# Differential heads gathered with the queries on the partitions, normed there and then transposed

## The chip, the core and the metric

The kernel runs on one core of a Trainium2 chip. The metric is the device time of one execution in microseconds (us), the median of several runs. All arithmetic is float32, with TensorE products made from pairs of rounded float32 parts.

## The reference

Three model blocks run on one sequence of 512 tokens with a width of 1024. The change lies in the second block, which has two layers; each layer is a feed-forward part, a mixer with attention, and another feed-forward part. The mixer has eight plain heads ("fox", eight of width 64, worked in four pairs) and four differential heads of width 128. What matters is this:

```python
p_d = jax.nn.softmax(s_d, axis=-1)
a_d = p_d[:, :, 0] - lam * p_d[:, :, 1]
o_d = jnp.einsum('bhqk,bhkd->bhqd', a_d, v_d)
...
o_d = _rmsnorm(o_d, subln) * (1.0 - lambda_init)
# y = x * rsqrt(mean(x * x, axis=-1) + 1e-5) * gain: the mean is over the 128 values of one head and one query
return jnp.concatenate([o_f, o_d], axis=-1) @ w_out
```

## The kernel before

The activations are held transposed: features on the 128 partitions, the 512 tokens along the free dimension. Each weight is loaded by DMA, rounded by ScalarE (L1579), and its remainder made by GpSimd (L2662); each product is then three matmuls (L1183 to L1185, `products`). The work is one order written out by hand: `program` calls the same sequence of steps on each engine, and each engine's class emits its own instructions of a step, with semaphore waits between the engines. So every engine has one queue in a fixed order, and a waiting instruction holds all that stands behind it on its engine.

PSUM is eight banks, and a step takes the bank that was taken or let go the longest time ago among those not held. `take` on an engine waits for the event `free` of the bank's former user. A bank that a head's output is gathered in (`('o', layer, 'd', i)`) is held from its first gather to its fourth and then let go, so that it goes to the end of the turn.

`attend` runs 32 jobs in each layer, a head and one of its four blocks of 128 queries: first the four differential heads, then the four pairs of fox heads. One pass of its loop emits, in this order, the scores of one job (L1484, L1487; two banks taken ahead of both), one gather, DVE's weighing of an earlier job, one turn (the transposes at L1497 and ScalarE's copy, L1879), and one step of `both()` (two for a pair). A step of `both()` is a step of `projections()` and then a step of `norms()`. A step of `projections()` is half a projection (`T_part`); behind the second half DVE evicts the projection with `fox_in` (L2502, L2503) or `diff_in`.

`norms()` norms the differential heads. Call the pass in which the fourth gather of head i is emitted **pass A**, and those behind it **B** and **C**. Before the change, a head goes so:

- Pass A: the gather (L1511) gives values on the partitions and queries along the bank. ScalarE copies the bank to `OD` (L1887) and frees it; then `diff_norm` j = 0, ScalarE's square of `OD` (L1901).
- Pass B: j = 1 (`roots`). TensorE sums the squares over the partitions with four matmuls of two columns (L1239), ScalarE takes the root (L1619), DVE the reciprocal (L2113). DVE's part stands behind `fox_in`.
- Pass C: j = 2 (`row`). TensorE spreads the result over all partitions with four matmuls of 128 columns (L1269), and ScalarE copies them out (L1634).
- The pass behind C: j = 3. DVE multiplies `OD` by the row and the gain (L2563) and by a constant (L2565).

Later ScalarE and DVE split `OD` into its rounded part and remainder (`diff_parts`), and the output projection reads them.

Of the kernel before, what the change touches and what calls it, by code (L numbers as in the profile page):

```python
# [7 lines left out]
ALU = mybir.AluOpType  # L8
# [733 lines left out]
def second(on, k, layer, before):  # L742
    L, A = (str(layer), before.A)
    scale = before.sum if layer else before.twin
    prior = ('added', 'f2_0', 7) if layer else ('final', 'fin1', 7)
    res = Residual('f1_' + L, lambda j: 0.5, banked(Sum('m' + L, k.R[1 - layer], S, prior, (), 2, [('lo', ('mid', 'f1_' + L), FF - 1)])), scale=scale, A=k.XA('m' + L), g=lambda j: param(k, 'mix_' + L, j))
    ffn(on, k, Ffn('f1_' + L, 'f1i' + L, 'f1o' + L, A, scale, res, [('filled', ('d', 'f2_0', 7))] if layer else [('filled', ('d', 'ff1', 7))], None if layer else before, iter(()) if layer else before.side))
    last = ('filled', ('d', 'f1_' + L, 7))
    A, R = (res.A, res.sum)
    on.mix_loads(L, last)  # L750
    on.T2((('ff', L), 'ff' + L, 0), (('dqk', L, 0), 'dqk' + L, 0), A)
    on.roots(R, 2)
    on.T(('dqk', L, 4), 'dqk' + L, 4, A)
    on.row(R, hold=True)
    on.diff_in(L, 0, R, last)
    on.diff_in(L, 4, R, last)
    on.forget(L, R, last)
    for kp in range(4):
        on.K(('dv', L), 'dv' + L, 0, A, kp, 4)
        if kp in (1, 2):  # L760
            on.rope(L, 4 * kp - 4)
    for tt in range(4):
        on.mix_value(L, 'dv', k.DV, tt, R, last)
    for n in (1, 5):
        on.T(('dqk', L, n), 'dqk' + L, n, A)
        on.diff_in(L, n, R, last)
    on.mix_lambda(L, layer)
    for kp in range(4):
        on.K(('fv', L), 'fv' + L, 0, A, kp, 4)
        if kp < 2:  # L770
            on.rope(L, 4 * kp + 1)
    for tt in range(4):
        on.mix_value(L, 'fv', k.FV, tt, R, last)
    at = Heads(k, L, [('d', i) for i in range(4)] + [('f', i) for i in range(4)], k.P2, [last, ('lambda', L), ('forgot', L)])
    at.OA, at.lam, at.scale = (Pair('oa' + L, k.OAH, k.OAL), k.sm[:, 68:69], 1.0 - (0.8 - 0.6 * math.exp(-0.3 * layer)))
    at.old = [('filled', ('s', L, ('d', 3), 3, 1)), ('filled', ('o', L, 'd', 3))]
    at.cleared = ('lo', 'oa' + L, 7)
    res = Residual('out2_' + L, lambda j: 1.0, banked(Sum('f2_' + L, k.R[layer], S, ('added', 'f1_' + L, 7), (1, 3, 5, 7), 0, [('filled', ('out2_' + L, 0))])), A=k.XA('f2_' + L), g=lambda j: param(k, 'ffn2_' + L, j))

    def projections():  # L780

        turn = None
        for n in (2, 6, 3, 7):
            on.T_part(('dqk', L, n), 'dqk' + L, n, A, 0, 2)
            if turn is not None:
                on.rope(L, turn)
            yield
            on.T_part(('dqk', L, n), 'dqk' + L, n, A, 1, 2)
            on.diff_in(L, n, R, last)
            turn = n  # L790
            yield
        for n in (0, 4, 1, 5, 2, 6, 3, 7):
            on.T_part(('fqk', L, n), 'fqk' + L, n, A, 0, 2)
            if n == 0:
                on.rope(L, turn)
            yield
            on.T_part(('fqk', L, n), 'fqk' + L, n, A, 1, 2)
            on.fox_in(L, n, R, last)
            yield
        yield  # L800
        for i in range(4):
            on.diff_parts(at, i)
            if i % 2:
                yield
        for n in range(KT):
            on.T(('outd_' + L, n), 'out' + L, n, at.OA, kt=4, first=4)
            on.part(res, n, ('outd_' + L, n))
            yield
            yield

    def norms():

        for i in range(4):
            while at.out <= i:
                yield
            for j in range(4):
                on.diff_norm(at, j, i)
                yield

    def both():  # L820
        one, two = (projections(), norms())
        while next(one, 'end') != 'end':
            next(two, None)
            yield
    attend(on, at, both())
    for n in range(KT):
        on.T(('out2_' + L, n), 'out' + L, n, at.OA, kt=4)
        on.residual(res, n, ('out2_' + L, n), ('filled', ('fqk', L, 7)))
    A = res.A
    scale = res.sum  # L830
    nxt = banked(Sum('fin2' if layer else 'f1_1', k.R[1 - layer], S, ('fox', L, 7), range(8) if layer else (), 2, [('lo', ('mid', 'f2_' + L), FF - 1)]))
    if layer:
        twin = banked(Sum('n3', k.R[2], S, None, range(8)))
        twin.slots = nxt.slots
        res = Residual('f2_1', lambda j: 0.5, nxt, scale=scale, twin=twin, by='final2')
    else:
        res = Residual('f2_0', lambda j: 0.5, nxt, scale=scale, A=k.XA('f1_1'), g=lambda j: param(k, 'ffn1_1', j))
    ffn(on, k, Ffn('f2_' + L, 'f2i' + L, 'f2o' + L, A, scale, res, [('filled', ('out2_' + L, 7))]))
    return res
# [291 lines left out]
class Tensor(Engine):  # L1131
# [368 lines left out]
    def gather(self, at, h, qt):  # L1500

        k, e = (self.k, self.e)
        key, outs = (at.bank(h), at.outs(h, qt))
        bo = self.take(k.banks, *key, hold=True) if qt == 0 else self.bank(*key)
        for name, weights, place in outs:
            self.wait_ge('turned', name)
        for event in at.ready(h):
            self.wait_ge(*event)
        for kt in range(qt + 1):
            for c, (name, weights, (a, z)) in enumerate(outs):  # L1510
                m = e.matmul(bo[a:z, qt * 128:qt * 128 + 128], at.value(h, kt, c), at.T.of(name)[:, kt * 128:kt * 128 + 128], start=kt == 0, stop=kt == qt)  # L1511
        m.then_inc(*k.filled.inc(*[('free', name) for name, weights, place in outs], *([('filled', key)] if qt == 3 else [])))
        if qt == 3:
            k.banks.let(key)

    def diff_norm(self, at, j, i):
        sq = diff_sum(at, i)
        if j == 1:
            self.roots(sq, 2, 8.0)
        if j == 2:  # L1520
            self.row(sq)

    def lru(self, s, n, w=0):
        k, e = (self.k, self.e)
# [26 lines left out]
def conv_sum(k):  # L1551
    return Sum('cn', k.R[1], S, ('oscaled', 3), range(8))


def diff_sum(at, i):
    sq = Sum(('hn', at.tag, i), at.N.of(('hn', at.tag, i)))
    sq.last = 0
    return sq


class Scalar(Engine):
# [319 lines left out]
    def head_out(self, at, h):  # L1881
        k, e, key = (self.k, self.e, at.bank(h))
        kind, i = h
        if kind == 'd':
            self.wait_ge('filled', key)
            self.wait_ge('load', 'cum', at.tag)
            e.copy(k.OD[:, i, :], self.bank(*key)).then_inc(*k.act.inc(('od', at.tag, i), ('free', key)))  # L1887
        if kind == 'f':
            self.high(at.OA, i, self.bank(*key), ('filled', key), *at.old, *([at.cleared] if i > 1 else []))
        if kind == 'm':  # L1890
            pass
# [3 lines left out]

    def diff_norm(self, at, j, i):
        k, e = (self.k, self.e)
        if j == 0:
            m = self.take(at.N, 'hn', at.tag, i)
            self.wait_ge('od', at.tag, i)  # L1900
            e.activation(m, k.OD[:, i, :], ACT.Square).then_inc(*k.act.inc(('ssq', ('hn', at.tag, i), 0)))  # L1901
        if j == 1:
            self.roots(diff_sum(at, i), 2, 8.0)
        if j == 2:
            self.row(diff_sum(at, i))

    def diff_parts(self, at, i):
        self.high(at.OA, 4 + i, self.k.OD[:, i, :], ('diff normed', at.tag, i), *at.old)
# [124 lines left out]
class Vector(Engine):  # L2033
# [424 lines left out]
    def mix_lambda(self, L, layer):  # L2458
        k, e, o = (self.k, self.e, COL['lam_' + L][0])
        for j in range(2):  # L2460
            e.tensor_tensor(k.sm[:, 64 + j:65 + j], k.col[:, o + 2 * j:o + 2 * j + 1], k.col[:, o + 2 * j + 1:o + 2 * j + 2], ALU.mult).then_inc(*k.dve.inc(*([('lam products', L)] if j else [])))
        lam = k.sm[:, 68:69]
        self.wait_ge('lam exp', L)
        e.tensor_tensor(lam, k.sm[:, 67:68], k.sm[:, 66:67], ALU.subtract).then_inc(*k.dve.inc())
        self.settle()
# [89 lines left out]

    def diff_norm(self, at, j, i):
        k, e = (self.k, self.e)
        x, tag = (k.OD[:, i, :], ('hn', at.tag, i))
        if j == 1:
            self.roots(diff_sum(at, i), 2, 8.0)  # L2560
        if j == 3:
            self.wait_ge('row', tag)
            e.scalar_tensor_tensor(x, x, param(k, 'subln_' + at.tag), diff_sum(at, i).acc, ALU.mult, ALU.mult).then_inc(*k.dve.inc(('free', tag)))  # L2563
            self.settle()
            e.tensor_scalar(x, x, at.scale, None, ALU.mult).then_inc(*k.dve.inc(('diff normed', at.tag, i)))  # L2565

    def diff_parts(self, at, i):
        self.low(at.OA, 4 + i, self.k.OD[:, i, :])
# [266 lines left out]
```

## Time and profile before

| | |
|---|---|
| Runs | 3512.21, 3517.94, 3516.43 us; median 3516.43 us |
| Profiled execution | 3512.08 us, with a span of 3510.4 us from first to last instruction |
| Busy, share of the span | TensorE 98%, TensorE weight load 79%, DVE 35%, ScalarE 36%, GpSimd 42% |
| Chain that ended last | TensorE 93%, DVE 2%, ScalarE 2%, DMA 1%, issue 1%, GpSimd 1% |
| Heads of the first layer | head 0 copied out at 1719.8 us, head 3 at 1787.4 us |
| Heads of the second layer | head 0 copied out at 2725.1 us, head 3 at 2792.7 us |

A row of the timeline gives the start in us, the duration in us, the engine, the line, the operation, the output and input, and how many instructions were merged. In brackets stands how long the engine sat idle before it, and what released it. PE is TensorE's matmul part, PEld its weight load, ACT is ScalarE, POOL is GpSimd, `ps` is a PSUM bank and `t` a tile in SBUF. A float32 matmul at L1239, L1269 and L1511 leaves two records each, a transpose at L1497 one. The end of a TensorE record is modelled and overlaps the next one; from start to start is the true pace.

### The profile page before, as it was taken

The page shows a single profiled execution, that of the slowest core. Times are in us where ns is not written, and L with a number is a line of the kernel's source. Part 1 is how long each engine was busy: PE and PEld are TensorE (multiplying, and loading weights), DVE is VectorE, ACT ScalarE, POOL GpSimd, SP SyncE. Part 2 cuts the span into 40 slices and gives each one's busy share as a digit, 9 for nine tenths or more (in the row PEclk, how much of TensorE's full clock was granted, in tenths as well). Part 3 has the DMA queues.
Part 4 walks back from the last instruction along what each step waited for, and adds up shares of the span by engine and source line. Part 5 has one row for each costly group of instructions (what it writes and reads, how often), then busy time and mean ns, then how long its engine had stood idle before and what let it go on. Part 6 is the DMA issues. An engine that isn't in the chain of part 4 may idle for free.

```text
span 3510.4 us, 39172 instructions
## 1 busy us (share of the span) xinstructions
PE 3442.5 (98%) x16124; PEld 2774.4 (79%) x16124; DVE 1236.9 (35%) x2137; ACT 1255.6 (36%) x1924; POOL 1471.6 (42%) x672
## 2 busy tenths in 40 slices
PE   8999999999999999999999999999999999999998
PEld 5777887887888887887777888888887778888776
DVE  3265784533111144212553111111113652111544
ACT  4524323433322332223454222322223553222544
POOL 4222444554544444445423444444445224444332
PEclk9999999999999999999999999999999999999999
DMA  7211223442333323333112223233332122223211
GB/s 269 70 51 55 90 97 111 153 150 73 126 132 120 102 96 132 135 94 108 55 34 96 99 95 95 88 105 98 94 96 88 33 76 95 97 90 102 72 60 55
DMA packets 99294, 341.19 MB, mean 97 GB/s; under 512 B 11371, under 2 KB 11755, under 8 KB 98956
## 3 DMA queue, kind: packets, MB, share of 16 engines
q1 hardware_dynamic: 98352, 336.97, 28.9%
q8 instruction: 128, 2.10, 0.3%
q10 hardware_dynamic: 764, 1.72, 0.1%
q14 instruction: 50, 0.41, 0.0%
HBM read 336.02 MB, written 2.10 MB: 96 GB/s over the span
## 4 chain that ended last, share of the span: by engine, by line
PE 93%; DVE 2%; ACT 2%; DMA 1%; issue 1%; POOL 1%; SPq 0%; DVEq 0%; ACTq 0%
PE ps L1183 26%; PE ps L1185 25%; PE ps L1184 25%; PE ps L1202 2%; PE ps L1204 2%; PE ps L1203 2%; PE ps L1484 2%; PE ps L1511 1%; PE ps L1497 1%; PE ps L1399 1%; PE ps L1269 1%; POOL t L2662 1%; PE ps L1413 0%; PE ps L1239 0%; DMA t<-in_w_ada 0%
## 5 line engine op out<-in xcount | busy, mean ns | idle before, releaser
L2662 POOL TENSOR_TENSOR t<-t,t 128x1024 fp32r<-128x1024 f32 (+2 forms) x588 | 1361.2, 2317 | 1925.3 <-ACT t L1579 1924.3
L1183 PE MATMUL ps<-t,t 128*128 128x512 f32 (+1 forms) x4048 | 1607.7, 397 | 17.4 <-POOL t L2662 8.6
L1185 PE MATMUL ps<-t,t 128*128 128x512 f32 (+1 forms) x4048 | 1583.9, 391 | 0.0
L1184 PE MATMUL ps<-t,t 128*128 128x512 f32 (+1 forms) x4048 | 1579.7, 390 | 0.0
L1183 PEld LDWEIGHTS ps<-t,t 128*128 128x128 f32 x4048 | 764.0, 189 | 184.8 <-issue 17.5
L1185 PEld LDWEIGHTS ps<-t,t 128*128 128x128 f32 x4048 | 763.2, 189 | 167.5
L1184 PEld LDWEIGHTS ps<-t,t 128*128 128x128 f32 x4048 | 764.1, 189 | 157.9 <-issue 1.4
L1579 ACT CAST t<-t 128x1024 fp32r<-128x1024 f32 (+2 forms) x588 | 584.3, 995 | 571.6 <-PE ps L1185 416.3
L2455 DVE TENSOR_TENSOR t<-t,ps 128x512 f32<-128x512 f32 x110 | 75.7, 688 | 531.7 <-PE ps L1185 516.9
L1648 ACT CAST t<-t 128x512 fp32r<-128x512 f32 x158 | 97.0, 621 | 401.4 <-DVE t L2455 361.5
L1835 ACT ACTIVATE t<-t 128x512 f32<-128x512 f32 x88 | 55.6, 632 | 315.1 <-DVE t L2448 315.0
L2047 DVE TENSOR_TENSOR t<-t,t 128x512 fp32r<-128x512 f32 x138 | 120.1, 875 | 119.7 <-ACT t L1648 119.7
L2290 DVE SCALAR_TENSOR_TENSOR ps<-t,t,ps 128x392 f32<-128x392 f32 (+14 forms) x232 | 159.0, 685 | 6.2
L2416 DVE TENSOR_TENSOR t<-ps,t 128x512 f32<-128x512 f32 x32 | 22.1, 692 | 381.5 <-PE ps L1185 381.5
L2448 DVE TENSOR_TENSOR t<-ps,t 128x512 f32<-128x512 f32 x88 | 60.7, 690 | 251.4 <-PE ps L1185 225.5
L1202 PE MATMUL ps<-t,t 128*128 128x512 f32 x336 | 137.3, 409 | 6.6 <-DVE t L2151 3.9
L1872 ACT ACTIVATE t<-ps,t 128x128 f32<-128x128 f32 (+3 forms) x160 | 86.5, 545 | 151.7 <-PE ps L1497 66.2
L1204 PE MATMUL ps<-t,t 128*128 128x512 f32 x336 | 132.9, 396 | 0.0
L1203 PE MATMUL ps<-t,t 128*128 128x512 f32 x336 | 132.7, 395 | 0.0
L2511 DVE TENSOR_REDUCE t<-ps 128x1 f32<-128x128 f32 (+3 forms) x160 | 77.6, 485 | 72.9 <-PE ps L1487 71.8
L1817 ACT ACTIVATE t<-t,t 128x512 fp32r<-128x512 f32 x48 | 34.7, 723 | 157.2 <-DVE t L2418 107.5
L2099 DVE SCALAR_TENSOR_TENSOR t<-t,t,t 128x1024 f32<-128x1024 f32 x49 | 77.2, 1575 | 31.5 <-DMA t<-in_w_ada 31.4
(285 smaller groups left out, 2283.2 us busy)
## 6 DMA issues: line engine op xcount, KB each, us to landing
t<-in_w_f1i SPq DMA_DIRECT2D x88, 512.0 KB, 3.3
t<-in_w_f2i SPq DMA_DIRECT2D x88, 512.0 KB, 3.3
t<-in_w_ada SPq DMA_DIRECT2D x72, 512.0 KB, 4.4
t<-in_w_ffi SPq DMA_DIRECT2D x44, 512.0 KB, 3.7
t<-in_w_f1o SPq DMA_DIRECT2D x32, 512.0 KB, 3.6
t<-in_w_f2o SPq DMA_DIRECT2D x32, 512.0 KB, 3.5
t<-in_w_gate SPq DMA_DIRECT2D x24, 512.0 KB, 4.0
t<-in_w_out SPq DMA_DIRECT2D x48, 256.0 KB, 2.6
```

Of the source, the lines that this page charges most:

```text
L1183: e.matmul(out, wh[:, at], X.hi[c][:, 0:N], start=c == first, stop=False)
L1184: e.matmul(out, wh[:, at], X.lo[c][:, 0:N], start=False, stop=False)
L1185: m = e.matmul(out, wl[:, at], X.hi[c][:, 0:N], start=False, stop=c == final)
L1202: e.matmul(out, X.hi[c][:, at], wh[:, w], start=c == 0, stop=False)
L1203: e.matmul(out, X.hi[c][:, at], wl[:, w], start=False, stop=False)
L1204: m = e.matmul(out, X.lo[c][:, at], wh[:, w], start=False, stop=c == 7)
L1579: e.copy(k.WH[:, n % NHL, 0:w], k.raw[:, j % NRAW, 0:w]).then_inc(*k.rounded.inc(('rounded', j)))
L1648: e.copy(A.hi[t], src).then_inc(*k.act.inc(('hi', A.tag, t)))
L1872: e.activation(p[:, 0:n], self.bank('s', *key)[:, 0:n], ACT.Exp, scale=at.root(h, qt, c) if h[0] == 'm' else 0.125, bias=st[:, 1:2], accum ...
L2047: e.tensor_tensor(A.lo[t], src, f(A.hi[t]), ALU.subtract).then_inc(*k.dve.inc(('lo', A.tag, t), *events))
L2290: e.scalar_tensor_tensor((c3 if j == 30 else a3)[:, :, lo:hi], h3[:, :, lo + w - 15:hi + w - 15], param(k, 'conv_w', w * 8 + i), a3[:, :, ...
L2662: e.tensor_tensor(k.WL[:, n % NHL, 0:w], k.raw[:, j % NRAW, 0:w], f(k.WH[:, n % NHL, 0:w]), ALU.subtract).then_inc(*k.rest.inc(('rest', j) ...
```

## The change

The gather of a differential head swaps its two operands, so that the queries are on the partitions and the 128 values of the head along the bank. The sum of squares of one query then runs along the free dimension: in pass A, instead of the copy, ScalarE makes four squares, one for each block of 128 queries, with an accumulated output, and takes the root at j = 0. In pass B (j = 1), where TensorE has no work any more, DVE takes the reciprocal and multiplies the PSUM bank by it into the scratch tile; this instruction frees the bank. In pass C (j = 2) TensorE transposes the scratch tile with four transposes, and ScalarE copies the result to `OD`, with the gain times the constant as its scale, once the load `cum` is done. The step j = 3 is gone. The product of gain and constant is one more small DVE instruction in each layer.

```diff
@@ second: norms()
-            for j in range(4):
+            for j in range(3):
@@ Tensor.gather
-                m = e.matmul(bo[a:z, qt * 128:qt * 128 + 128], at.value(h, kt, c), at.T.of(name)[:, kt * 128:kt * 128 + 128], start=kt == 0, stop=kt == qt)
+                turned, values = (at.T.of(name)[:, kt * 128:kt * 128 + 128], at.value(h, kt, c))
+                held, moved = (turned, values) if h[0] == 'd' else (values, turned)
+                m = e.matmul(bo[a:z, qt * 128:qt * 128 + 128], held, moved, start=kt == 0, stop=kt == qt)
@@ Tensor.diff_norm
-        sq = diff_sum(at, i)
-        if j == 1:
-            self.roots(sq, 2, 8.0)
+        k, e, tag = (self.k, self.e, ('hn', at.tag, i))
         if j == 2:
-            self.row(sq)
+            b, m = (self.take(k.banks, 'turned out', at.tag, i), at.N.of(tag))
+            self.wait_ge('od scaled', at.tag, i)
+            for t in range(4):
+                x = e.transpose(b[:, t * 128:t * 128 + 128], m[:, t * 128:t * 128 + 128], const(k, 'ident'))
+            x.then_inc(*k.filled.inc(('filled', ('turned out', at.tag, i)), ('free', tag)))
@@ Scalar.head_out
         if kind == 'd':
+            m, c = (self.take(at.N, 'hn', at.tag, i), self.take(k.cols, 'cols', ('hn', at.tag, i)))
             self.wait_ge('filled', key)
-            self.wait_ge('load', 'cum', at.tag)
-            e.copy(k.OD[:, i, :], self.bank(*key)).then_inc(*k.act.inc(('od', at.tag, i), ('free', key)))
+            for t in range(4):
+                w = slice(t * 128, t * 128 + 128)
+                e.activation(m[:, w], self.bank(*key)[:, w], ACT.Square, accum_out=c[:, t:t + 1]).then_inc(*k.act.inc())
@@ Scalar.diff_norm
+        tag = ('hn', at.tag, i)
         if j == 0:
-            m = self.take(at.N, 'hn', at.tag, i)
-            self.wait_ge('od', at.tag, i)
-            e.activation(m, k.OD[:, i, :], ACT.Square).then_inc(*k.act.inc(('ssq', ('hn', at.tag, i), 0)))
-        if j == 1:
-            self.roots(diff_sum(at, i), 2, 8.0)
+            c = k.cols.of(('cols', tag))[:, 0:4]
+            self.settle()
+            e.activation(c, c, ACT.Sqrt, scale=1.0 / 128, bias=unit(k, 2)).then_inc(*k.act.inc(('root', tag)))
         if j == 2:
-            self.row(diff_sum(at, i))
+            self.wait_ge('filled', ('turned out', at.tag, i))
+            self.wait_ge('load', 'cum', at.tag)
+            e.activation(k.OD[:, i, :], self.bank('turned out', at.tag, i), ACT.Copy, scale=k.sm[:, 69:70]).then_inc(*k.act.inc(('diff normed', at.tag, i), ('free', ('turned out', at.tag, i))))
@@ Vector.mix_lambda
+        e.tensor_scalar(k.sm[:, 69:70], param(k, 'subln_' + L), 1.0 - (0.8 - 0.6 * math.exp(-0.3 * layer)), None, ALU.mult).then_inc(*k.dve.inc())
@@ Vector.diff_norm
-        x, tag = (k.OD[:, i, :], ('hn', at.tag, i))
+        tag, key = (('hn', at.tag, i), at.bank(('d', i)))
         if j == 1:
-            self.roots(diff_sum(at, i), 2, 8.0)
-        if j == 3:
-            self.wait_ge('row', tag)
-            e.scalar_tensor_tensor(x, x, param(k, 'subln_' + at.tag), diff_sum(at, i).acc, ALU.mult, ALU.mult).then_inc(*k.dve.inc(('free', tag)))
+            c = k.cols.of(('cols', tag))[:, 0:4]
+            self.wait_ge('root', tag)
+            e.reciprocal(c, c).then_inc(*k.dve.inc())
             self.settle()
-            e.tensor_scalar(x, x, at.scale, None, ALU.mult).then_inc(*k.dve.inc(('diff normed', at.tag, i)))
+            e.tensor_tensor(halves(at.N.of(tag)), halves(self.bank(*key)), c.rearrange('p (a n) -> p a n', n=1).broadcast_to([128, 4, 128]), ALU.mult).then_inc(*k.dve.inc(('od scaled', at.tag, i), ('free', key), ('free', ('cols', tag))))
```

`settle` makes an engine wait for its own last instruction.

## Rows read from the trace of the kernel before

**Rows 1.** The page: busy time, share of the span and instructions of each engine.

```profile
PE 3442.5 (98%) x16124; PEld 2774.4 (79%) x16124; DVE 1236.9 (35%) x2137; ACT 1255.6 (36%) x1924; POOL 1471.6 (42%) x672
```

**Rows 2.** Windows: stretch, length, busy PE, PEld, DVE, ACT, POOL, TensorE clock, DMA.

```profile
1720.00:1735.00 15.00, 15.00 (x86) 11.16 (x86) 8.60 (x24) 9.50 (x19) 6.37 (x4) 1.00 0.12 36
```

**Rows 3.** Timeline: head 0 of layer 0, pass B, TensorE and DVE.

```profile
1726.48 0.39 PE L1185 MATMUL ps<-t,t 128*128 128x512 f32 x1
1726.71 0.95 PE L1239 MATMUL ps<-t,t 128*128 128x2 f32 x8
1726.91 0.68 DVE L2502 TENSOR_TENSOR t<-ps,t 64x512 f32<-64x512 f32 x1
1727.58 0.92 PE L1484 MATMUL ps<-t 64*128 64x384 f32 x4
1727.62 0.69 DVE L2503 TENSOR_TENSOR t<-ps,t 64x512 f32<-64x512 f32 x1
...
1728.34 0.20 DVE L2113 RECIPROCAL t<-t 128x8 f32<-128x8 f32 x1
```

**Rows 4.** Timeline: the row of head 0, then a turn of eight transposes.

```profile
1732.23 1.05 PE L1269 MATMUL ps<-t,t 128*128 128x128 f32 x8
...
1733.21 1.13 PE L1484 MATMUL ps<-t 64*128 64x512 f32 x4
...
1823.04 1.04 PE L1497 MATMUL ps<-t,t 128*128 128x128 f32 x8
...
1823.91 1.88 PE L1484 MATMUL ps<-t,t 80*128 80x512 f32 x4
```

**Rows 5.** Lines by form, 1700 to 1760 us: count, busy us, mean ns, idle before.

```profile
L2495 DVE TENSOR_TENSOR t<-ps,t 128x512 f32<-128x512 f32 x3 | 2.1, 692 | 5.2 <-PE ps L1474 5.2
```

**Rows 6.** Timeline: a release of TensorE by DVE in the third block.

```profile
3471.73 0.35 DVE L2533 TENSOR_SCALAR t<-t,t 128x256 f32<-128x256 f32 x1
...
3472.13 0.55 PE L1497 MATMUL ps<-t,t 128*128 128x128 f32 x3 [1.01 <-DVE t L2533]
```

**Rows 7.** Timeline: head 0 of layer 0, pass A, ScalarE.

```profile
1719.45 0.36 ACT L1872 ACTIVATE t<-ps,t 128x128 f32<-128x128 f32 x1
...
1719.79 0.59 ACT L1887 COPY t<-ps 128x512 f32<-128x512 f32 x1
...
1720.26 0.39 ACT L1879 COPY t<-ps 128x256 f32<-128x256 f32 x1
```

**Rows 8.** Timeline: head 3 of layer 0, passes B and C.

```profile
1794.66 0.20 DVE L2113 RECIPROCAL t<-t 128x8 f32<-128x8 f32 x1 [6.80 <-ACT t L1619]
...
1795.01 1.13 PE L1269 MATMUL ps<-t,t 128*128 128x128 f32 x8 [0.22 <-DVE t L2527]
...
1796.13 1.28 ACT L1872 ACT_TABLE_LOAD   x1 [1.50 <-DVE t L2517]
...
1798.14 1.53 PE L1484 MATMUL ps<-t,t 80*128 80x384 f32 x4 [1.34 <-ACT t L1872]
```

**Rows 9.** Timeline: TensorE's first matmuls behind waits elsewhere in the kernel.

```profile
1330.10 0.77 PE L1183 MATMUL ps<-t,t 128*128 128x512 f32 x1 [2.96 <-POOL t L2662]
...
1882.42 0.77 PE L1183 MATMUL ps<-t,t 128*128 128x512 f32 x1 [1.75 <-POOL t L2662]
...
1885.95 0.40 PE L1185 MATMUL ps<-t,t 128*128 128x512 f32 x1
...
2887.76 0.50 PE L1183 MATMUL ps<-t,t 128*128 128x512 f32 x1 [1.74 <-POOL t L2662]
...
3275.80 0.50 PE L1183 MATMUL ps<-t,t 128*128 128x512 f32 x1 [2.12 <-POOL t L2662]
...
3478.43 0.88 PE L1511 MATMUL ps<-t,t 128*64 128x128 f32 x12 [2.09 <-ACT t L1879]
```

**Rows 10.** Windows of TensorE alone: stretch, length, busy, clock, DMA share, GB/s.

```profile
1884.00:1886.00 2.00, 2.00 (x7) 0.53 0.53 207
...
3480.00:3482.00 2.00, 1.23 (x10) 0.50 0.02 4
```

More of the change, by code:

```diff
@@ L774, in second @@
     at = Heads(k, L, [('d', i) for i in range(4)] + [('f', i) for i in range(4)], k.P2, [last, ('lambda', L), ('forgot', L)])
-    at.OA, at.lam, at.scale = (Pair('oa' + L, k.OAH, k.OAL), k.sm[:, 68:69], 1.0 - (0.8 - 0.6 * math.exp(-0.3 * layer)))
+    at.OA, at.lam = (Pair('oa' + L, k.OAH, k.OAL), k.sm[:, 68:69])
     at.old = [('filled', ('s', L, ('d', 3), 3, 1)), ('filled', ('o', L, 'd', 3))]
@@ L1552, in conv_sum @@
     return Sum('cn', k.R[1], S, ('oscaled', 3), range(8))
[L1555 to L1558, printed above, removed]
 class Scalar(Engine):
```

## The prediction

> **What bounds the kernel now.** I read the page's busy times first. TensorE is busy for 98% of the span [rows 1], so the kernel is as long as TensorE's queue: an instruction taken off it is a gain of its pace, a wait put into it is a loss, and work on the other engines costs only where TensorE waits for it. Then I read the stretch of the differential heads by windows: TensorE 15.00 of 15.00 us busy at full clock, DVE 8.60, ScalarE 9.50 [rows 2]. The cover is complete there, so the norm costs today just what TensorE itself spends on it. Third came the timeline of one head, for the places in each queue. The eight heads (two layers of four) repeat one pattern; rows 3, 4 and 7 show head 0 of layer 0, and head 3 of a layer differs, as told below.
>
> **TensorE's own work.** Pass B loses the four two-column matmuls: from 1726.71 to the next scores at 1727.58, 0.87 us [rows 3]. In pass C the row takes 1733.21 - 1732.23 = 0.98 us, and eight transposes take 1823.91 - 1823.04 = 0.87, so four take 0.43 [rows 4]: -0.55. The gather has as many matmuls of 128x128 by 128 columns with its operands swapped: 0. If nothing waited, the change would give 8 x (0.87 + 0.55) = 11.4 us.
>
> Of the transposes a rule speaks against this. The Trainium skill (TensorE: Matmul & The Clock Gate, Part 4: PE-mode transpose) gives about 275 ns for one in a kernel; taken as a pace, four would cost 1.10 us by an estimate from that page and the new pass C would be no shorter than the old. The rows have eight in 0.87 us, because records overlap, so the sum keeps 0.43.
>
> **The bank's release.** Here is the new wait. Before, ScalarE's copy freed the output bank in pass A. Now DVE's product in pass B frees it. I followed the turn of the eight banks through the passes by the rule of the kernel: one of the eight is held by a projection and, from pass B on, one by the next head's output; between the fourth gather and the scores of pass C a head's passes take six or seven (a turn, a projection and for head 0 a rotation in A, two scores, the output and a turn in B), and in the old order the two-column matmuls took one more, for head 0 the freed bank itself. That taker is gone, so for heads 0, 1 and 2 the next taker of the output bank is one of the two score banks of pass C, and TensorE takes both ahead of its first scores matmul. Those scores are the very next thing in TensorE's queue behind the projection's last matmul, while DVE must first evict that projection (two `fox_in` instructions), then take the reciprocal, settle and multiply. All other engines' work stays behind TensorE's wait, and TensorE has nothing to run meanwhile.
>
> The wait, from head 0 [rows 3]: the projection's last matmul starts at 1726.48; TensorE reaches the scores at about 1726.71. DVE starts `fox_in` at 1726.91 and the reciprocal at 1728.34, ready at 1728.54. The product reads 512 columns from PSUM: nearest is DVE's product from PSUM of the same shape, 0.69 us [rows 5]. With 0.04 for settling it ends at 1729.27. DVE releases TensorE in 3472.13 - (3471.73 + 0.35) = 0.05 [rows 6]. So the scores start at 1729.33, against 1727.58 today: **+1.75 us** for each of these heads, with the 0.87 already counted in it. TensorE stands idle from 1726.48 + 0.39 to 1729.33, some 2.5 us. Below, the product can't be under the 0.35 of DVE's short product at L2533 [rows 6]: +1.4; above, nothing shown is over 0.2 more: +1.95.
>
> Six such heads: 6 x 1.75 = +10.5. Pass C of all eight: 8 x -0.55 = -4.4.
>
> **Head 3.** Its bank is next taken by its own transposes, which wait for the same product anyway: no new wait. It loses the 0.87. And today DVE stands 6.80 us at its reciprocal, since ScalarE's root comes late behind the turn copies; through that, the next `Exp` with its table load of 1.28 comes late and TensorE waits 1.34 at the scores, and 0.22 before the row [rows 8]. With the root moved to pass A, right behind the squares, DVE isn't held: both waits go. Two heads: 2 x -(0.87 + 1.34 + 0.22) = -4.9. If what is late next (the turn copies, which wait for the gather) keeps 1.34, it is only -2.2.
>
> **ScalarE.** The copy takes 1720.26 - 1719.79 = 0.47 of its queue; four squares from PSUM with an accumulator are nearest to the `Exp` of 128 columns, 1719.79 - 1719.45 = 0.34 apart [rows 7]: 1.36, so +0.9. Bounds are 0.34 each or, not overlapped, 0.36 plus an accumulator read of some 0.2: up to 2.2. The weight rounding and the turn copies behind it come 0.9 us later. The copy is first wanted by a gather two passes on, and the rounding by a projection two weights on, each several us away: 0, and 1 us a head if that cover fails. The root's table load moves with the root from B to A and the reload for `Exp` from C to B, both beside TensorE; the count stays. From 1719.79 the squares, a turn copy and a rounding (together under 3 us) and the load and root (1.28 and some 0.3) make the root ready by about 1724.5, and DVE comes to it at 1728.34: 0. The scaled copy in pass C replaces the row's copy: 0. `cum` is loaded long before: 0.
>
> **DVE and the rest.** The two products of j = 3, about 1.2 us a head, go from DVE, which is not the bound: 0. The extra scalar product in `mix_lambda` is 0. No DMA is added or moved, on SP's or any other queue, and GpSimd's queue keeps its instructions.
>
> Sum so far: 10.5 - 4.4 - 4.9 = **+1.2 us**.
>
> **The clock.** A TensorE that stands idle comes back at half clock in some places. Behind 1.75 us it ran from 1882.42 to 1885.95 for eight matmuls that at full pace (0.23 apart, [rows 3]) take 1.84: 1.7 us lost [rows 9], and the granted clock is 0.53 there, the 1.2 GHz level [rows 10]. So it was behind 2.09 (clock 0.50, [rows 9, 10]) and 2.96. Behind 1.74 and 2.12 it kept 2.4 GHz: first matmul 0.50 long instead of 0.77 [rows 9]. The idle time here is 2.5, between these; three of the five fell, and both that kept it were shorter. I take four of six: 4 x 1.7 = +6.8. Bounds are none (0) and six (+10.2).
>
> **Sum.** 1.2 + 6.8 = +8.0 us. The profiled execution took 3512.08 us, 4.35 below the median 3516.43, so the change would put it at 3520.1 and the median at **3524.4 us**. The measurement can tell about 0.2%, 7.0 us.
>
> **Rivals.**
> - *Clock kept at most of the six waits* (three drops at the most): +1.2 to +6.3, 3517.6 to 3522.7. For it: 2.12 us of idle time did not lower the clock. Against it: 1.75 did. 0.28.
> - *No wait at the scores*: the product has freed the bank by the time that TensorE comes, or the score banks of pass C are others than I count. Then all the gains stand: -11.4 - 2 x 1.56 = -14.5, 3501.9. It decides where the product ends before the projection's last matmul, 2.5 us sooner than I place it. For it: DVE is only 35% busy and loses work. Against it: `fox_in` can't start before TensorE's last projection matmul, and the product stands behind it. 0.13.
> - *Longer chain on DVE*: the product, with its repeated operand, takes twice the 0.69, or ScalarE's root comes later than `fox_in`. 6 x 0.7 = +4.2 and the clock falls six times: 1.2 + 4.2 + 10.2 = +15.6, 3532.0. DVE is not pressed otherwise there; 0.08.
> - *It evens out*: only some heads wait, or head 3's gain is larger, and the time is within 3 us of before, 3513.4 to 3519.4. 0.08.
>
> That leaves 0.43 for the forecast, four to six drops, +8.0 to +11.4.
>
> **How the numbers follow.** Slower by over 0.2%: the forecast and the longer chain, 0.51. Same: clock kept, and evened out, 0.36. Faster: 0.13. The range leaves out the case without a wait and the tail of the longer chain, and reaches from a partial wait (3513) to a long chain (3532).
>
> **What would show it.** In passes B to C of heads 0 to 2 of both layers, TensorE's L1484 waits about 2.5 us for DVE's product, with the two `fox_in` in front of it; the matmuls behind show 0.63 instead of 0.40 where the clock fell. At head 3, the waits of 1.34 and 0.22 are gone. Four transposes take 0.43. No turn copy or weight is waited for anew. The prediction is wrong if L1484 shows no such wait; if its wait is there and the time is the same, the clock was the step that failed.

## The result, and the profile after

The kernel after takes **3525.23 us** (median of 15 runs, 3518.89 to 3532.61), the kernel before, run beside it 15 times, 3512.51 us (3507.09 to 3523.07). The ratio is 1.0034, with a 95% interval of 1.0024 to 1.0043: slower, by 12.7 us. The forecast was 3524.4 us as a time and +8.0 us as a difference; the median of before came out 3.9 lower with 15 runs than with the three that the forecast started from. The profiled execution of after took 3518.89 us, the fastest of its 15, so its trace should show somewhat less than the median loss.

The page of after, beside [rows 1]:

```profile
span 3517.3 us, 39012 instructions
PE 3438.7 (98%) x16028; PEld 2769.2 (79%) x16028; DVE 1225.5 (35%) x2131; ACT 1256.4 (36%) x1972; POOL 1470.9 (42%) x672
```

TensorE lost 96 records and 3.8 us of busy time, and the span grew by 6.9 us all the same. Busy time alone would call the change a gain; TensorE must stand idle for 10.7 us more. (Matmuls that run longer at a lower clock count as busy, so that price is hidden in the busy time.) The windows of the stretch of [rows 2] (all engines; columns as there) say so:

```profile
1720.00:1735.00 15.00, 12.21 (x58) 8.63 (x58) 8.95 (x23) 7.51 (x16) 5.71 (x4) 0.89 0.11 35
```

TensorE was busy for 15.00 of these 15 us and is now for 12.21, at a granted clock of 0.89 in place of 1.00. Which wait it is, the waits of TensorE in layer 0, from 1683 to 1856 us, tell (engine, line waited at, releaser: us in total, times, longest us):

```profile
PE ps L1484 <- DVE t L2567: 5.3, 2, 2.8
PE ps L1484 <- DVE t L2530: 2.5, 1, 2.5
PE ps L1513 <- ACT t L1878: 0.9, 1, 0.9
PE ps L1183 <- DVE t L2049: 0.8, 1, 0.8
PE ps L1484 <- ACT t L1871: 0.4, 1, 0.4
```

L1484 are the scores, L2567 is DVE's new product. The releaser of the third wait is named L2530, an instruction of the weighing right behind the product; that wait is at the same place in its head's passes, and in r2, r3, r4 and r7 below it comes, goes and changes its length with the other two (in r3, r7 and r9 it is the product itself that is named). The place in the queues, timeline of head 0 (compare [rows 3], where the scores started at 1727.58 without a wait):

```profile
1725.64 0.67 DVE L2505 TENSOR_TENSOR t<-ps,t 64x512 f32<-64x512 f32 x1
1726.35 0.69 DVE L2506 TENSOR_TENSOR t<-ps,t 64x512 f32<-64x512 f32 x1
1727.07 0.18 DVE L2565 RECIPROCAL t<-t 128x4 f32<-128x4 f32 x1
1727.29 0.69 DVE L2567 TENSOR_TENSOR t<-ps,t 128x512 f32<-128x512 f32 x1
1728.03 1.25 PE L1484 MATMUL ps<-t 64*128 64x384 f32 x4 [2.79 <-DVE t L2567]
...
1751.04 0.92 PE L1484 MATMUL ps<-t 64*128 64x384 f32 x4 [2.53 <-DVE t L2567]
...
1774.13 1.53 PE L1484 MATMUL ps<-t,t 80*128 80x384 f32 x4 [2.53 <-DVE t L2530]
...
2736.74 0.92 PE L1484 MATMUL ps<-t 64*128 64x384 f32 x4 [2.79 <-DVE t L2567]
...
2758.15 0.92 PE L1484 MATMUL ps<-t 64*128 64x384 f32 x4 [2.52 <-DVE t L2567]
...
2781.25 1.53 PE L1484 MATMUL ps<-t,t 80*128 80x384 f32 x4 [2.52 <-DVE t L2530]
```

That is the chain of the forecast: two `fox_in`, reciprocal, product, and TensorE starts 0.05 behind the product's end (1727.29 + 0.69 = 1727.98). There are six such waits, three in each layer, 15.7 us together. The first of each layer is 0.26 longer than the others, since DVE comes to `fox_in` late: it starts 0.78 behind the start of the projection's last matmul (1724.86), where at head 2 it starts 0.43 behind it. The windows behind them (TensorE alone; columns as in [rows 10]) give the clock:

```profile
1728.00:1730.00 2.00, 1.97 (x9) 0.62 0.00 0
1754.00:1756.00 2.00, 2.00 (x7) 0.55 0.00 0
1775.00:1777.00 2.00, 2.00 (x15) 1.00 0.04 8
2738.00:2740.00 2.00, 2.00 (x14) 1.00 0.00 0
2761.00:2763.00 2.00, 2.00 (x6) 0.57 0.00 0
2784.00:2786.00 2.00, 2.00 (x7) 0.50 0.00 0
```

At four the clock fell to the lower level, 1.2 GHz, and at two it stayed at 2.4 GHz, behind 2.53 and 2.79 us of idle time.

TensorE's shorter work and head 3, beside [rows 4] and [rows 8]:

```profile
1734.29 0.60 PE L1524 MATMUL ps<-t,t 128*128 128x128 f32 x4
1734.81 1.13 PE L1484 MATMUL ps<-t 64*128 64x512 f32 x4
...
1796.22 0.18 DVE L2565 RECIPROCAL t<-t 128x4 f32<-128x4 f32 x1 [2.29 <-ACT t L1903]
...
1801.48 1.53 PE L1484 MATMUL ps<-t,t 80*128 80x384 f32 x4 [0.42 <-ACT t L1871]
```

Four transposes take 1734.81 - 1734.29 = 0.52 us, where the row took 0.98. At head 3 DVE waits 2.29 for the root instead of 6.80, TensorE's 0.22 is gone, and of its 1.34 a wait of 0.42 is left.

**The account.** From the first scores matmul of a layer to its last is the stretch in which the two kernels differ. The lines of L1484 by form, of after, give its ends (duration min/median/max in ns, first to last start):

```profile
L1484 PE MATMUL ps<-t x64: 272/481/813, 1680.3 to 1758.4; 64*128 64x128 f32 x16, 64*128 64x256 f32 x16, 64*128 64x384 f32 x16, 64*128 64x512 f32 x16
L1484 PE MATMUL ps<-t,t x64: 272/433/595, 1762.6 to 1850.2; 80*128 80x128 f32 x16, 80*128 80x256 f32 x16, 80*128 80x384 f32 x16, 80*128 80x512 f32 x16
```

Taken to 0.01, the two layers have 169.83 and 169.81, 339.6 us together, and before 164.83 and 164.86, 329.7. So the stretches give +10.0. By its parts: six waits +15.7; eight times (0.87 + 0.98 - 0.52), taken off, -10.6; head 3, 2 x -(0.92 + 0.22) = -2.3; four falls at 1.7, +6.8. Sum +9.6, 0.4 short of what was seen.

### The profile page after: what moved, and what is told of

It reads as the page before. It is cut to its first block, busy times and chain, and to the rows that moved or that the text cites. A ratio compares the mean times of both kernels' runs of the same rounds, so it can differ in the third digit from the quotient of the medians.

```text
span 3517.3 us, 39012 instructions
## 1 busy us (share of the span) xinstructions
PE 3438.7 (98%) x16028; PEld 2769.2 (79%) x16028; DVE 1225.5 (35%) x2131; ACT 1256.4 (36%) x1972; POOL 1470.9 (42%) x672
## 4 chain that ended last, share of the span: by engine, by line
PE 93%; DVE 2%; ACT 2%; issue 1%; POOL 1%; DMA 1%; SPq 0%; DVEq 0%; ACTq 0%
PE ps L1183 26%; PE ps L1185 25%; PE ps L1184 25%; PE ps L1202 2%; PE ps L1484 2%; PE ps L1203 2%; PE ps L1204 2%; PE ps L1513 2%; PE ps L1497 1%; PE ps L1399 1%; POOL t L2664 1%; PE ps L1413 0%; PE ps L1269 0%; DMA t<-in_w_ada 0%; PE ps L1487 0%
## 5 line engine op out<-in xcount | busy, mean ns | idle before, releaser
L1183 PE MATMUL ps<-t,t 128*128 128x512 f32 (+1 forms) x4048 | 1608.1, 397 | 15.3 <-POOL t L2664 6.4
L1183 PEld LDWEIGHTS ps<-t,t 128*128 128x128 f32 x4048 | 764.6, 189 | 181.7 <-issue 13.7
```

What stands on the lines that cost most here:

```text
L1183: e.matmul(out, wh[:, at], X.hi[c][:, 0:N], start=c == first, stop=False)
```

## Experiments

Times are medians of several executions over five rounds, beside the kernel before; the ratio is to it, as it ran in the same rounds (medians of 3512.2, 3512.1 and 3514.3 us). "Clock" is the mean granted clock, and "stretch" the sum over both layers as above, both from the profiled execution.

| Run | median us | ratio, 95% | span us, clock | stretch us |
|---|---|---|---|---|
| before | 3512.51 | 1 | 3510.4, 0.990 | 329.7 |
| after | 3525.23 | 1.0034, 1.0024 to 1.0043 | 3517.3, 0.989 | 339.6 |
| r1_after_again | 3524.97 | 1.0039, 1.0026 to 1.0052 | 3525.8, 0.987 | 342.9 |
| r2_late_turn | 3498.07 | 0.9960, 0.9947 to 0.9972 | 3495.0, 0.991 | 316.6 |
| r3_kept_busy | 3514.38 | 1.0013, 1.0001 to 1.0025 | 3512.9, 0.991 | 332.9 |
| r4_longer_product | 3531.76 | 1.0054, 1.0040 to 1.0068 | 3535.6, 0.986 | 347.3 |
| r5_norm_first | 3513.06 | 0.9999, 0.9990 to 1.0008 | 3509.4, 0.990 | 330.1 |
| r6_late_root | 3511.51 | 0.9994, 0.9984 to 1.0004 | 3507.9, 0.988 | 323.1 |
| r7_busy_half | 3518.89 | 1.0021, 1.0010 to 1.0031 | 3519.2, 0.989 | 336.1 |
| r8_twice_turned | 3504.61 | 0.9974, 0.9965 to 0.9982 | 3506.4, 0.989 | 320.2 |
| r9_vector_first | 3497.96 | 0.9961, 0.9948 to 0.9973 | 3504.1, 0.989 | 321.8 |
| r10_late_turn_again | 3496.59 | 0.9957, 0.9943 to 0.9970 | 3494.0, 0.991 | 316.6 |

Span less stretch, which the edits leave all but untouched, is 3180.7 before, 3177.6 in after and lies between 3177.4 and 3188.3 in these single executions. Nearly all of that is the clock: half of the time that each trace has at the lower level outside the stretches is 31 to 41 us, and with it taken off 3145 to 3149 us are left in all twelve. A stretch is therefore the finer measure for an edit, and a median can differ from it by some us through falls of the clock elsewhere.

**r1_after_again.** The kernel after, unchanged.

> The changed kernel again, as the measure beside the others of this chip. My theory (the scores of pass C wait 2.5 us for DVE's product at heads 0 to 2 of both layers, and the clock falls behind most of these waits): 12 us over the kernel before, ratio 1.003 to 1.004. The rival that the earlier difference was mostly scatter between runs: under 1.002.

It repeats: 3524.97. Its six waits have the same lengths to 0.01, but the clock fell behind all six. At the sixth (scores at 2787.00) it fell later than at the others, in this window of TensorE alone:

```profile
2788.00:2792.00 4.00, 4.00 (x17) 0.60 0.00 0
```

So which waits are followed by a fall differs from execution to execution of one kernel, with the same idle times. The stretch, 3.3 us longer than in after, is the price of two more falls, at 1.7 each.

**r2_late_turn**, and **r10_late_turn_again**, the same kernel once more. The bank goes to the end of the turn a second time in pass B, where its last reader now stands. No instruction changes; only who takes which bank.

```diff
@@ Tensor.diff_norm
+        if j == 1:
+            k.banks.let(at.bank(('d', i)))
```

> Only the turn of the PSUM banks differs from the changed kernel: in pass B the output bank is put at the end of the turn once more, so that the scores of pass C take banks that have long been free. No instruction is added or removed. Theory (the wait for the bank is the whole loss): no wait of L1484 for DVE's product; against the kernel before 8 x -0.52 (transposes for the row) + 8 x -0.87 (two-column matmuls) + 2 x -1.14 (waits of head 3) = -13.4 us, ratio 0.996, 25 us under the changed kernel. Rival (the loss is the ScalarE squares or the moved root, which hold up other work): the wait goes to another line and the ratio stays over 1.

> The kernel of r2 again, to see how far its gain repeats: r6 and r8 lay 3 to 7 us higher above r2 than their attention stretches account for. Theory (r2's repair is worth 13 us over the kernel before): ratio 0.995 to 0.997. Rival (r2 was low by some 5 us through the clock elsewhere): 0.9975 or more.

3498.07 and 3496.59 us: faster than before by 0.4%, and than after by 0.8%. The waits of TensorE in layer 0 of r2:

```profile
PE ps L1513 <- ACT t L1880: 0.9, 1, 0.9
PE ps L1183 <- DVE t L2051: 0.8, 1, 0.8
PE ps L1484 <- ACT t L1873: 0.3, 1, 0.3
```

The three waits for DVE are gone and nothing took their place. Timeline of its head 0 (its stretch begins at 1683.8, that of after at 1680.3), and the window of [rows 2]:

```profile
1728.68 0.92 PE L1484 MATMUL ps<-t 64*128 64x384 f32 x4
...
1730.79 0.69 DVE L2569 TENSOR_TENSOR t<-ps,t 128x512 f32<-128x512 f32 x1
...
1733.35 0.60 PE L1526 MATMUL ps<-t,t 128*128 128x128 f32 x4
```

```profile
1720.00:1735.00 15.00, 15.00 (x81) 10.62 (x80) 10.94 (x32) 10.08 (x29) 4.91 (x4) 1.00 0.11 36
```

The scores start 2.8 us before the end of the product that they waited for in after. It ends at 1731.48, still 1.9 us ahead of the transposes. DVE's chain is no shorter; TensorE just no longer asks for that bank. The stretch is 23.0 shorter than in after: the waits 15.7, four falls 6.8, and 2 x (0.4 - 0.3) account for 22.7. This shows that the whole loss lies in the bank's turn.

**r3_kept_busy** and **r7_busy_half.** These tell the clock's part from the wait's. (The diff is r3's; in r7 the loop is over `range(1)`.) In pass B of heads 0 to 2 TensorE makes two matmuls (r3), or one (r7), of the identity into a free bank, which nothing reads. They fill part of the idle time and do not shorten the wait for the bank.

```diff
@@ Tensor.diff_norm
+        if j == 1 and i < 3:
+            s = k.banks
+            n = next(n for n in s.turn if n not in s.held and n != s.at[at.bank(('d', i))])
+            self.wait_ge('free', s.key[n])
+            for t in range(2):
+                e.matmul(s.aps[n], const(k, 'ident'), k.con[:, 0:512], start=True, stop=True)
```

> The changed kernel with two needless float32 matmuls of 512 columns (0.86 us each) in TensorE's queue in pass B of heads 0 to 2, into a free bank, just ahead of the wait for the product. They fit into the wait, so its end doesn't move; what is left is 0.8 us of idle time. Theory (the idle time lowers the clock, 1.7 us at each of four to six places): the granted clock stays at full speed behind the waits and the time falls by 7 to 10 us against the changed kernel, to a ratio of 1.0005 to 1.0015. Rival (the clock costs nothing or falls anyway): the same time as the changed kernel.

> As r3, with one needless matmul (0.86 us) instead of two, which leaves 1.6 to 1.9 us of idle time. Theory (whether the clock falls hangs on how long TensorE is idle): it falls behind some of the six waits, so the time lies between r3 and the changed kernel, ratio 1.0015 to 1.0035. Rival (any wait over a microsecond lowers it, or none under 2.5): the time of the changed kernel, or that of r3.

With two, idle times are 1.07, 0.72 and 0.72, and the clock stays up (the first wait, and the window behind it):

```profile
1729.18 0.92 PE L1484 MATMUL ps<-t 64*128 64x384 f32 x4 [1.07 <-DVE t L2573]
```

```profile
1730.00:1735.00 5.00, 5.00 (x32) 1.00 0.00 0
```

Useless work makes the kernel 10.6 us faster than r1 (stretch -10.1, six falls being 10.2). Against the profiled execution of after the stretch is 6.8 shorter, and four falls are 6.8. The scores are released by the same product in all three, so this difference is the clock's alone. That none of the six waits lowers it is shown for the profiled execution; four of r3's eleven executions took 3521 to 3527 us, at a granted clock of 0.987 to 0.989, and where it was low in them is not known. With one matmul the idle times are 1.93, 1.57 and 1.58; the clock fell behind the first of layer 0 (1.93, the window below) and the last of layer 1 (1.57) and held behind four, and the median lies between.

```profile
1732.00:1734.00 2.00, 2.00 (x11) 0.50 0.00 0
```

In these runs, a fall followed 1.57 us and none followed 2.79 us: the length of one wait does not decide it. It matters all the same: in the profiled executions a fall followed 16 of the 18 waits of 2.52 to 3.52 us at the scores of after, r1 and r4, two of the six of 1.57 to 1.93 in r7, and none of those of up to 1.34 in r3 and r9.

**r4_longer_product.** DVE makes the product twice.

```diff
@@ Vector.diff_norm
+            e.tensor_tensor(..., ALU.mult).then_inc(*k.dve.inc())
+            self.settle()
             e.tensor_tensor(..., ALU.mult).then_inc(*k.dve.inc(('od scaled', at.tag, i), ('free', key), ('free', ('cols', tag))))
```

> The changed kernel with DVE's product done twice in each of the eight heads (0.69 us more and 0.04 to settle). Theory (TensorE waits for the end of DVE's chain): each of the six waits is 0.73 longer, +4.4 us and up to two more falls of the clock, +3.4: 4 to 8 us over the changed kernel, ratio 1.0045 to 1.0060. Rival (the scores wait for something else, as ScalarE's late work): under 1 us more.

```profile
1736.19 0.95 PE L1484 MATMUL ps<-t 64*128 64x384 f32 x4 [3.52 <-DVE t L2569]
...
1783.72 1.91 PE L1484 MATMUL ps<-t,t 80*128 80x384 f32 x4 [3.25 <-DVE t L2530]
```

Each wait is 0.73 or 0.72 longer, the product's 0.69 and a settling of 0.03. Six make 4.4, and the stretch is 4.4 longer than in r1, with six falls in both. DVE is 35% busy, and yet each us put on it at this place is a us of the kernel. The third wait, too, grew with the product, whatever line its releaser is put down to. The median is 6.8 above r1; the other 2.4 are not explained by the stretch.

**r5_norm_first.** On all engines a step of `norms()` comes ahead of the step of `projections()`, so that DVE's product stands ahead of `fox_in`.

```diff
@@ second: both()
-        while next(one, 'end') != 'end':
+        while True:
             next(two, None)
+            if next(one, 'end') == 'end':
+                break
             yield
```

> The changed kernel with the step of the norm ahead of the step of the projection in each pass, so that DVE's product stands in front of the two fox_in instead of behind them; the banks go as in the changed kernel. Theory (the wait is DVE's order in pass B): the scores' wait shrinks from 2.5 us by the two evictions' 1.4 to 1.1 and the clock stays up behind it: 6 x 1.4 = 8 us and the clock's 7 to 10 us less than the changed kernel, ratio to the kernel before 0.998 to 0.9995. Rival (the product is held by ScalarE's root, so its place doesn't matter): the wait stays at 2.5 us.

3513.06, level with before, and less gained than expected. The waits did not shrink alike: 2.94, 1.77 and none, in both layers. Nor did the clock stay up, as I had expected: it fell behind the 1.77 of layer 0 and the 2.94 of layer 1 (0.57 in 1754 to 1758 and in 2737 to 2741 us). Shorter waits (6.3) and two falls in place of four (3.4) make 9.7 us, and the stretch is 9.5 shorter than in after. ScalarE now takes its root ahead of the weight rounding, GpSimd's remainder of that weight starts later, and it lands beside DVE's weighing. Timeline of DVE and GpSimd, head 0:

```profile
1728.59 1.28 POOL L2720 TENSOR_TENSOR t<-t,t 128x512 f32<-128x512 f32 x1
...
1728.64 1.25 DVE L2543 TENSOR_TENSOR t<-t 128x1 f32<-128x1 f32 x1
...
1729.92 1.44 DVE L2545 SCALAR_TENSOR_TENSOR t<-t,t,t 128x128 f32<-128x128 f32 x1
1729.95 1.26 POOL L2723 TENSOR_TENSOR t<-t,t 128x512 f32<-128x512 f32 x1
...
1731.48 0.69 DVE L2569 TENSOR_TENSOR t<-ps,t 128x512 f32<-128x512 f32 x1
1732.22 0.92 PE L1486 MATMUL ps<-t 64*128 64x384 f32 x4 [2.94 <-DVE t L2569]
```

The remainder of the weight (L2666) runs from 1726.23 to 1728.63, some 1.5 us later than in after, both counted from the first scores of the layer. A DVE instruction on one element a partition takes 1.25 us, and ends at 1729.89, just as GpSimd's does at 1729.87. The next one, L2545, starts at 1729.92 beside GpSimd's of 1729.95 and ends at 1731.36, 0.15 behind it. The Trainium skill (SBUF — State Buffer, Terms) has a rule for it: DVE and GpSimd share one pair of ports, held for a whole instruction, and the loser "fully blocks"; the trace agrees for these two, to 0.15 us. Not every DVE instruction is held: a TENSOR_SCALAR of 128x1 at 1726.36 kept its 0.15 us inside GpSimd's L2666.

**r9_vector_first.** The same swap on DVE alone; ScalarE and TensorE keep their order, and so do the weights.

```diff
@@ second: both()
+        while isinstance(on, Vector):
+            next(two, None)
+            if next(one, 'end') == 'end':
+                return
+            yield
```

> As r5, but only DVE's order is changed: its reciprocal and product stand ahead of the two fox_in, while ScalarE's queue keeps the order of the changed kernel, so that the weight rounding and GpSimd's remainder behind it stay where they were. In r5 GpSimd ran beside DVE's weighing and the weighing took up to 2.4 us. Theory (that overlap, brought by ScalarE's order, is why r5 gained little): the waits at the scores are 1.1 to 1.4 us at heads 0 to 2 and the two layers' attention takes 8 us less than in the changed kernel and the clock stays up; ratio 0.998 to 1.000. Rival (DVE's weighing is late in any case): waits of 1.8 to 2.9 us as in r5.

```profile
1729.70 0.92 PE L1489 MATMUL ps<-t 64*128 64x384 f32 x4 [1.34 <-DVE t L2572]
...
1768.37 1.53 PE L1489 MATMUL ps<-t,t 80*128 80x384 f32 x4 [0.53 <-DVE t L2572]
```

The bank's turn is as in after, the waits are 1.34, none for DVE (0.30 for ScalarE), and 0.53, and the clock stays up. 3497.96 us, more gained than expected. So the loss needed both: a bank asked for early, and a product behind two evictions. Its stretch of 321.8 is 5.2 above r2's; the medians of the two are alike all the same. r9's five executions had granted clocks of 0.989 to 0.993 and r2's 0.990 to 0.991, 5 us less lost by span times one less the clock, and that makes up for it; whether this is chance is not shown.

**r6_late_root** (on top of r2). ScalarE's root goes back from pass A to pass B.

```diff
@@ Scalar.diff_norm
-        if j == 0:
+        if j == 1:
```

> The kernel of r2 with ScalarE's root in pass B instead of A, as in the kernel before. Theory (the moved root is what took the waits of head 3 away): at head 3 DVE stands some 6 us at the reciprocal again and TensorE waits 1.3 us at the scores, 2 x 0.9 to 2 x 1.3 = 2 to 3 us more than r2, ratio 0.9965 to 0.997. Rival (head 3's gain comes from the row and the two-column matmuls alone): the same time as r2.

Head 3 of layer 0:

```profile
1788.43 0.18 DVE L2567 RECIPROCAL t<-t 128x4 f32<-128x4 f32 x1 [5.94 <-ACT t L1905]
...
1789.48 0.63 PE L1526 MATMUL ps<-t,t 128*128 128x128 f32 x4 [0.96 <-DVE t L2532]
...
1792.44 1.56 PE L1484 MATMUL ps<-t,t 80*128 80x384 f32 x4 [1.67 <-ACT t L1873]
```

DVE's long wait is back (5.94 beside 6.80 in [rows 8]), the 1.34 is back as 1.67, and 0.96 at the transposes is new: I had expected 2 to 3 us and had not counted that one. The stretch is 6.5 longer than r2's: 2.4 in layer 0, which is what the waits make (0.96 + 1.67 less r2's 0.3), and 4.0 in layer 1, where they are the same and the clock fell once behind the 1.67, at 1.7 a fall. The window of TensorE alone:

```profile
2795.00:2798.00 3.00, 3.00 (x18) 0.50 0.00 0
```

So the early root is what helps head 3. The median is 13.4 above r2, far over the range that I had set. Some 7 of that lie outside the stretches. In the profiled executions the rest is 6.5 longer than r2's, and half of the time at the lower clock there is 8.3 longer, so this is the clock elsewhere; whether moving the root brings it about is not shown.

**r8_twice_turned** (on top of r2). Each head's four transposes are made twice, for the price of a transpose.

```diff
@@ Tensor.diff_norm
-            for t in range(4):
+            for t in (0, 1, 2, 3, 0, 1, 2, 3):
```

> The kernel of r2 with the four transposes of each head done twice. Theory (a transpose costs TensorE 0.11 us of its pace): 32 more transposes, 3.5 us over r2, ratio 0.997. Rival (a transpose costs the 275 ns of its duration): 8.8 us over r2, ratio 0.9985.

```profile
1735.46 1.04 PE L1526 MATMUL ps<-t,t 128*128 128x128 f32 x8
1736.42 1.13 PE L1484 MATMUL ps<-t 64*128 64x512 f32 x4
```

Eight take 0.96, so the second four cost 0.44, and the stretch grew by 3.6, with 8 x 0.44 = 3.5. A transpose costs TensorE 0.11 us here; four with the step around them 0.52. The median is 6.5 above r2, 3 more than the stretch says; in the profiled execution the clock outside the stretches cost 6.5 more than in r2.

## Why the prediction was right

**The bank's release held as worked out.** It named the wait, its releaser, the instructions in front of it and the heads that have it. The time was put at 2.5 us of idle time, six times; it is 2.79 twice and 2.52 or 2.53 four times. Measured as the prediction measured it, from start to start, the scores come 2.94 and 2.69 late, 16.6 in all, and less 6 x 0.87 that is 11.4 where the sum had 10.5; the 0.9 more is DVE's late start at the first wait of each layer (0.3 each) and some 0.07 at each of the others. r2 shows that this turn is the cause. The product's 0.69 and the release's 0.05, taken from [rows 5] and [rows 6], were the rows to go by.

**TensorE's own work.** -0.55 a head for pass C is -0.46, since four transposes take 0.52, not half of what eight take: 0.7 us less gained over eight heads. The row that speaks to the rule weighed there is that of L1524, by line (duration min/median/max in ns):

```profile
L1524 PE MATMUL ps<-t,t x32: 271/272/273, 1734.3 to 2808.8; 128*128 128x128 f32 x32
```

One transpose lasts 272 ns. That the Trainium skill (TensorE: Matmul & The Clock Gate, Part 4: PE-mode transpose) gives some 275 ns for one of bf16 values agrees with this duration, here of float32; as a pace it would be wrong, for in r8 the next one comes 0.11 behind.

**Head 3** gave 2 x (0.87 + 0.92 + 0.22) = 4.0 of the 4.9 forecast. The mechanism was right (DVE's 6.80 became 2.29), but the next `Exp` is still 0.42 late.

**ScalarE.** The squares were put 0.34 apart; they are 0.25 apart:

```profile
1718.17 0.28 ACT L1888 ACTIVATE t<-ps 128x128 f32<-128x128 f32 x1
...
1718.42 0.28 ACT L1888 ACTIVATE t<-ps 128x128 f32<-128x128 f32 x1
```

They cost 1.0 and not 1.36 of its queue, and the cover held: in layer 0 the waits at L1513 and L1183 are 0.9 and 0.8, as before. DVE finds the root ready for head 0.

**The clock is the mis-sized term, and its reason failed.** Four of six falls, +6.8, is what the profiled execution has, the fastest of the 15. But r1 has six, and the median of 15 runs is 12.7 above before, not 8.0. With the shown parts the waits and savings alone make 15.7 - 10.6 - 2.3 = +2.8, and six falls put the sum at +13.0, four at +9.6. That most executions have five or six is argued from this, and shown for one; the granted clocks speak for it, 0.986 to 0.989 in the 15 executions of after and 0.989 to 0.993 in those of before beside r1, which makes 13 us more at the lower clock on average (span times one less the clock, the mean of each 15). So the term should have been about +10.2, its upper bound.

The step "both that kept it were shorter", from which I took four, was wrong: 2.79 kept the clock and 1.57 lost it. And the five waits of [rows 9] were a thin choice. The trace of before has five more of over 1.7 us behind 800 us (3.22, 2.32, 2.45, 3.05 and 4.45), and at each of them the clock is at 0.50 or falls to it soon behind (0.50 from 818 to 820, from 3255 to 3257 and from 3434 to 3436 us, for instance). Eight of ten would have given five of six.

That the time came out within 0.8 us of the 3524.4 is in part luck: the difference was 4.7 larger than forecast, and before 3.9 faster than the median that the forecast started from. What stands is that falls follow these waits often, at 1.7 us each, and that without them (r3) the change would cost 2 us by the median and 3.2 by the stretch.

**The rivals.** No wait at the scores was priced at -14.5; r2 and r10 make just this kernel and come out 14.1 and 17.7 under the before of their own rounds, with stretches 13.1 shorter in both. "Longer chain" was priced at +15.6; r4, which builds its doubled product, has a stretch 17.6 longer than before. "Clock kept" is r3: a stretch 3.2 longer.

## What to carry to other kernels

When a change moves the last reader of a buffer to a later step, look at who takes that buffer next, not only at what the reader costs. In a turn that is written by age, the point at which a buffer is let go must move with its reader: two lines turned a loss of 0.34% into a gain of 0.4%. And where a wait on a nearly full TensorE can't be removed, count a possible fall of its clock beside it, from all the waits of that length that the trace has; moving the releasing instruction ahead of others on its own queue (r9) is worth nearly as much as removing the wait.

## What the runs showed that was not expected

- The clock's fall is not settled by one idle time: in one execution it held behind 2.53 and 2.79 us and fell behind 2.52, and in another kernel it fell behind 1.57. Filling part of the gap with matmuls that nobody reads paid 10.6 us.
- Some DVE instructions that work in SBUF alone stand still beside GpSimd: a TENSOR_TENSOR of 128x1 took 1.25 us in r5, where it takes 0.15 otherwise. The product that reads PSUM kept its 0.69 wherever it lay.
- The profiled executions differ outside the changed stretches by up to 11 us (two of the same kernel, after and r1, by 5.3), and nearly all of it is time at the lower clock. Where the stretch can be measured in the trace, it says more of a small edit than the median does, once its own falls are counted.
